# FFN gate and up projections with the weights stationary and the operand's two parts streamed side by side

## The chip, the cores and the metric

The kernel runs on one core of a Trainium2 chip. The metric is the device time of one execution, in microseconds (us). Three executions of the kernel before took 1697.11 to 1703.02 us, median 1700.94 us. The profiled execution, from which all rows below come, took 1709.87 us, with a span of 1708.0 us from the first to the last instruction.

## The reference, cut to what matters

256 tokens of 1024 channels go through two stacks of two layers each. The first stack's layer is an FFN, a mixer and a second FFN; the second stack's layer is a mixer and an FFN. So there are six FFNs. All of them compute, with `D = 1024` and `D_FF = 2816`:

```
def rms_norm(x, g):
    y = x * lax.rsqrt(jnp.mean(x * x, axis=-1, keepdims=True) + 1e-6)
    return y * g
def swiglu(x, w_in, w_out):
    gu = x @ w_in                      # 1024 x 5632
    g, u = jnp.split(gu, 2, axis=-1)
    return (jax.nn.silu(g) * u) @ w_out  # 2816 x 1024
x = x + 0.5 * swiglu(rms_norm(x, norm), w_in, w_out)   # factor 1 in the second stack
```

## The kernel before, in words

**Precision.** Every large product is made of three matmuls of the type fp32r. An operand a is split into a high part (a rounded copy) and a low part (what the copy lacks). The product of a and w is then a_hi w_hi + a_hi w_lo + a_lo w_hi (`product`, L1417; its three matmuls are L1420, L1421 and L1422).

**Weights.** They come as units of 128 x 2048 elements (1 MB) into three slots of `raw`, by SyncE's queue (`load`, L446, two DMAs to a unit). ScalarE makes the high part of a unit (`refill`, L688, one ACTIVATE, L693) and VectorE the low part (`refill`, L997, one TENSOR_TENSOR, L1000). TensorE then uses the unit and counts it in `unit_done`; a refill waits for that count and for the landing. A load into `raw` waits for the low part of the unit before (`w_lo_ready`).

**An FFN.** It has eleven steps, each for 256 of the 2816 hidden channels. A step uses three units: two hold the 256 gate and the 256 up columns for 512 input channels each (slots 2 and 0), the third 256 rows of the down weights (slot 1). In the kernel before the tokens are stationary: for each of two tiles of 128 tokens, each of eight chunks of 128 input channels is loaded as `xTh` or `xTl`, and 512 columns of weights (256 gate, 256 up) are streamed past. That is 48 matmuls of 512 columns to a step (`full_block`, L1453). The result lies in one PSUM bank per token tile, tokens on the partitions, so that the norm's factor `rstd` is one scalar per partition. ScalarE forms silu of the gate half (`silu`, L730, L731), VectorE multiplies it by the up half (`product`, L1040, L1042). The result must then be transposed for the down product: four transposes on TensorE (`turn`, L1486, L1491), into the first bank of the pair. ScalarE makes the high part of that (`product_hi`, L739, L741) and VectorE the low part (`product_lo`, L1049, L1052). The down product is 24 matmuls of 512 columns into the four banks `acc` (`down`, L1498; for the last step `last_down`, L1510).

**Order.** It is written out by hand on each engine. TensorE runs: the first gate and up block, then for j = 0 to 9 the block of step j+1 and the down product of step j, then the last down product. The turn of step j+1 is issued half way through the down product of step j. The banks `pg` form two pairs, which the steps use in turn. ScalarE and VectorE go through the same steps with their refills in between. At the start of an FFN ScalarE and VectorE also finish the operand `xT`, and ScalarE waits for `rstd` from GpSimd. SyncE issues the loads in the order of use, with some other loads at fixed steps of the first stack's first FFNs: before step 6 it loads the attention bias (`attention_bias`), to which GpSimd then adds a mask in sixteen instructions (L631).

Of the kernel before, what the change touches and what calls it, by code (L numbers as in the profile page):

```python
# [20 lines left out]
F32 = mybir.dt.float32  # L21
# [113 lines left out]
class Signals:  # L135


    def __init__(self, sem):
# [37 lines left out]
        self.ffn_sum_done = sem("ffn_sum_done")  # L176
        self.silu_ready = sem("silu_ready")
        self.act_ready = sem("act_ready")
        self.actT_tr = sem("actT_tr")
        self.actT_hi = sem("actT_hi")  # L180
        self.actT_lo = sem("actT_lo")
# [103 lines left out]
def build(nc, a, out):  # L285

    with ExitStack() as ctx:
        def sb(name, shape, dt=F32):
            return ctx.enter_context(nc.sbuf_tensor(name, shape, dt))

        def psum(name):
            return ctx.enter_context(nc.psum_tensor(name, [P, BANK], F32))
# [28 lines left out]
        rstd = sb("rstd", [P, TT])  # L321
        rfin = sb("rfin", [P, TT])
        rnext = sb("rnext", [P, TT])
        consts_a = sb("consts_a", [P, CA_COLS])

        shared = sb("shared", [P, TT * NA_H * T])
# [13 lines left out]


        sg, act = area(12288, TT, FB), area(12800, TT, FB)
        squared = area(12288, D)


# [46 lines left out]
        spread = nc.dram_tensor("rpb_spread", (GRID_W, DEPTH * NA_H, NA_DR * GRID_W), F32, kind="Internal").ap()  # L392

        causal = consts_b[:, CB_CAUSAL:CB_CAUSAL + T]

# [4 lines left out]
        def f32(ap):  # L400
            return ap.bitcast(F32)
# [32 lines left out]
        def unit(slot, rnd):  # L434

            return SLOTS * rnd + slot
# [246 lines left out]
        def _(act_e):  # L683
# [43 lines left out]
            def ffn(rnd, f, n, o):  # L727
                begin(rnd, n, o)

                def silu(t, par):  # L730
                    act_e.activation(sg[:, t, :], pg[par][t][:, 0:FB], ACT.Silu, scale=rstd[:, t:t + 1]).then_inc(s.silu_ready, 1)  # L731

                refill(0, rnd + 1)
                act_e.wait_ge(s.ffn_t0_done, STEPS * f + 1)
                silu(0, 0)
                act_e.wait_ge(s.unit_done, unit(1, rnd) + 4)
                silu(1, 0)

                def product_hi(j, par):  # L739
                    act_e.wait_ge(s.actT_tr, STEPS * f + j + 1)  # L740
                    act_e.activation(bTh[:, 2 * par:2 * par + 2, :], pg[par][0][:, :].rearrange("p (c n) -> p c n", c=2),  # L741
                                     ACT.Copy).then_inc(s.actT_hi, 1)

                with act_e.Fori(0, (STEPS - 1) // 2) as jj:
                    for par in range(2):
                        j = 2 * jj + par
                        product_hi(j, par)
                        refill(1, rnd + j + 1)
                        act_e.wait_ge(s.ffn_t0_done, STEPS * f + j + 2)
                        silu(0, 1 - par)  # L750
                        refill(2, rnd + j + 1)
                        act_e.wait_ge(s.unit_done, unit(0, rnd + j + 1) + 4)
                        silu(1, 1 - par)
                        refill(0, rnd + j + 2)
                product_hi(STEPS - 1, 0)
# [240 lines left out]
        def _(v):  # L996
# [40 lines left out]
            def ffn(rnd, f, n, o, factor, gain=None, next_gain=None):  # L1037
                begin(rnd, n, o, gain)

                def product(t, par, j):  # L1040
                    v.wait_ge(s.silu_ready, 2 * STEPS * f + 2 * j + t + 1)
                    v.scalar_tensor_tensor(act[:, t, :], pg[par][t][:, FB:2 * FB], rstd[:, t:t + 1], sg[:, t, :],  # L1042
                                           ALU.mult, ALU.mult).then_inc(s.act_ready, 1)

                refill(0, rnd + 1)
                product(0, 0, 0)
                product(1, 0, 0)

                def product_lo(j, par):  # L1049
                    v.wait_ge(s.actT_hi, STEPS * f + j + 1)  # L1050
                    part = slice(2 * par, 2 * par + 2)
                    v.tensor_tensor(bTl[:, part, :], pg[par][0][:, :].rearrange("p (c n) -> p c n", c=2),  # L1052
                                    f32(bTh[:, part, :]), ALU.subtract).then_inc(s.actT_lo, 1)

                with v.Fori(0, (STEPS - 1) // 2) as jj:
                    for par in range(2):
                        j = 2 * jj + par
                        product_lo(j, par)
                        refill(1, rnd + j + 1)
                        product(0, 1 - par, j + 1)  # L1060
                        refill(2, rnd + j + 1)
                        product(1, 1 - par, j + 1)
                        refill(0, rnd + j + 2)
                product_lo(STEPS - 1, 0)

                def add(t, n2):
                    if t == 1 and n2 == 1:
                        v.wait_ge(s.unit_done, unit(2, rnd + STEPS - 1) + 4)
                    else:
                        v.wait_ge(s.ffn_sum_done, 3 * f + 2 * t + n2 + 1)  # L1070
                    residual(t, n2, acc[2 * t + n2], factor)

                if not next_gain:
                    for t in range(TT):
# [341 lines left out]
        def _(pe):  # L1416
# [63 lines left out]
            def ffn(rnd, f, n, o, alone):  # L1480
# [5 lines left out]
                def turn(j, par):  # L1486

                    pe.wait_ge(s.act_ready, 2 * STEPS * f + 2 * j + 2)
                    for t in range(TT):
                        for c in range(2):  # L1490
                            tr = pe.transpose(pg[par][0][:, c * T + t * P:c * T + (t + 1) * P], act[:, t, c * P:(c + 1) * P], ident[:, :])  # L1491
# [6 lines left out]
                def down(j, par, slot, r, first):  # L1498

                    pe.wait_ge(s.actT_lo, STEPS * f + j + 1)  # L1500
                    split_ready(slot, r)
                    for t in range(TT):
                        for k in range(2):
                            for n2 in range(2):
                                mm = added(t, par, slot, n2, k, first and k == 0, False)
                        if t == 0:
                            turn(j + 1, 1 - par)
                    mm.then_inc(s.unit_done, 1)

                def last_down(slot, r):  # L1510
# [15 lines left out]
                def step(j, par, amid=None, first=False):  # L1526
                    full_block((2, 0), (rnd + j, rnd + j + 1), BANK, pg[1 - par], s.ffn_t0_done, amid=amid)
                    down(j, par, 1, rnd + j + 1, first)

                step(0, 0, {(0, 1): lambda: turn(0, 0)}, first=True)  # L1530
                with pe.Fori(0, (STEPS - 3) // 2) as jj:
                    step(2 * jj + 1, 1)
                    step(2 * jj + 2, 0)
                step(STEPS - 2, 1)
                last_down(2, rnd + STEPS - 1)

            def mixer_a(l):
# [396 lines left out]
```

## Time and profile before

| | before |
|---|---|
| median of 3 executions | 1700.94 us |
| profiled execution, its span | 1709.87 us, 1708.0 us |
| VectorE, ScalarE, GpSimd busy | 55%, 47%, 6% of the span |
| transposes of the FFN (L1491) | 264, 40.5 us busy |
| splits of weight units (L693, L1000) | 277 on each engine |
| DMA engines, mean rate | 54.9% of 16 engines' span, 181 GB/s |

A busy time is the union of the instructions' records. Matmul records are longer than the distance from one matmul to the next (a matmul of 512 columns has a record of 0.39 us, and the next starts 0.227 us after it), since they are pipelined: what a matmul costs is read from the starts in the timeline, not from its record. Instructions of SyncE and the issue of DMAs are not counted as busy.

### The profile page before, as it was taken

Reading aid. Unit: us, or ns where it says so; the run is one execution under the profiler, and the core shown is the slowest. Engines: PE = TensorE matmul, PEld = TensorE weight load, DVE = VectorE, ACT = ScalarE, POOL = GpSimd, SP = SyncE. Lnnn points to the kernel's source line nnn. Section 1 sums busy time; section 2 is a strip of 40 time slices with the busy share of each in tenths; the row PEclk is TensorE's granted clock in tenths of the full one; section 3 lists DMA queues with packets and bytes.
Section 4 is the critical chain, followed back from the end, with each engine's and each line's share of the span. In section 5 each row is a group of like instructions: output and inputs, shape, how many; then the busy total and the mean of one; then the engine's idle time right before and its main releaser. Section 6 shows DMA issues by size and latency. Waiting matters only on the chain.

```text
span 1708.0 us, 20654 instructions
## 1 busy us (share of the span) xinstructions
PE 1665.7 (98%) x7760; PEld 1374.9 (80%) x7760; DVE 946.6 (55%) x843; ACT 800.4 (47%) x896; POOL 108.2 (6%) x138
## 2 busy tenths in 40 slices
PE   6998999999999998999999999989999999999998
PEld 5887887888888887888888888878888888888886
DVE  4545555575454645464556554566655556665454
ACT  4443454545444543345454444466444446554443
POOL 2010000000000002000001000031100002110000
PEclk9999999999999999999999999999999999999999
DMA  8884553356565677545345675642566564356562
GB/s 257 297 227 151 193 182 125 124 175 198 194 196 173 200 256 212 188 165 183 137 139 157 216 251 172 217 129 99 161 197 198 178 210 129 105 166 209 184 195 88
DMA packets 209179, 308.87 MB, mean 181 GB/s; under 512 B 10400, under 2 KB 153504, under 8 KB 208480
## 3 DMA queue, kind: packets, MB, share of 16 engines
q1 hardware_dynamic: 208272, 305.18, 54.9%
q0 software_dynamic: 560, 1.84, 0.4%
q8 instruction: 40, 0.66, 0.2%
q10 hardware_dynamic: 288, 1.05, 0.2%
q14 instruction: 19, 0.16, 0.0%
HBM read 306.97 MB, written 2.88 MB: 181 GB/s over the span
## 4 chain that ended last, share of the span: by engine, by line
PE 92%; DVE 3%; ACT 1%; DMA 1%; issue 1%; POOL 1%; SPq 0%; DVEq 0%; POOLq 0%; ACTq 0%
PE pg L1420 19%; PE pg L1422 19%; PE pg L1421 19%; PE acc L1420 8%; PE acc L1422 8%; PE acc L1421 8%; PE pg L1491 2%; DVE wlo L1000 2%; DMA raw<-in_ffn_w_in 1%; PE acc L1570 1%; PE pg L1433 1%; ACT whi L693 1%; PE acc L1590 1%; PE acc L1578 0%; PE acc L1610 0%
## 5 line engine op out<-in xcount | busy, mean ns | idle before, releaser
L1000 DVE TENSOR_TENSOR wlo<-raw,whi 128x2048 fp32r<-128x2048 f32 x277 | 646.3, 2334 | 522.0 <-ACT whi L693 522.0
L693 ACT ACTIVATE whi<-raw 128x2048 fp32r<-128x2048 f32 x277 | 529.5, 1914 | 355.5 <-PE acc L1422 165.7
L1420 PE MATMUL pg<-whi,xTh 128*128 128x512 f32 (+1 forms) x1456 | 578.2, 397 | 12.8 <-DVE wlo L1000 8.4
L1422 PE MATMUL pg<-whi,xTl 128*128 128x512 f32 (+1 forms) x1456 | 568.5, 390 | 0.0
L1421 PE MATMUL pg<-wlo,xTh 128*128 128x512 f32 (+1 forms) x1456 | 568.4, 390 | 0.0
L1420 PEld LDWEIGHTS pg<-whi,xTh 128*128 128x128 f32 x1456 | 274.9, 189 | 74.2 <-DVE wlo L1000 11.4
L1422 PEld LDWEIGHTS pg<-whi,xTl 128*128 128x128 f32 x1456 | 274.8, 189 | 57.2
L1421 PEld LDWEIGHTS pg<-wlo,xTh 128*128 128x128 f32 x1456 | 275.1, 189 | 54.1
L1420 PE MATMUL acc<-whi,bTh 128*128 128x512 f32 (+1 forms) x572 | 230.5, 403 | 0.0
L1422 PE MATMUL acc<-whi,bTl 128*128 128x512 f32 (+1 forms) x572 | 224.5, 392 | 0.0
L1421 PE MATMUL acc<-wlo,bTh 128*128 128x512 f32 (+1 forms) x572 | 224.0, 392 | 0.0
L731 ACT ACTIVATE work<-pg,rstd 128x256 f32<-128x256 f32 x132 | 62.1, 474 | 237.0 <-PE pg L1422 236.9
L1422 PEld LDWEIGHTS acc<-whi,bTl 128*128 128x128 f32 x572 | 108.2, 189 | 23.4
L1420 PEld LDWEIGHTS acc<-whi,bTh 128*128 128x128 f32 x572 | 108.6, 190 | 20.7 <-DVE bTl L1182 0.5
L1421 PEld LDWEIGHTS acc<-wlo,bTh 128*128 128x128 f32 x572 | 108.5, 190 | 20.5
L1042 DVE SCALAR_TENSOR_TENSOR work<-pg,rstd,work 128x256 f32<-128x256 f32 x132 | 62.9, 481 | 90.3 <-ACT work L731 90.3
L603 POOL TENSOR_TENSOR ms<-ss,eps 128x1 f32<-128x1 f32 x24 | 25.3, 1053 | 1140.9 <-ACT work L700 1140.9
L741 ACT ACTIVATE bTh<-pg 128x512 fp32r<-128x512 f32 x66 | 39.6, 601 | 81.0 <-PE pg L1491 81.0
L706 ACT ACTIVATE xTh<-pg 128x512 fp32r<-128x512 f32 x48 | 28.3, 597 | 58.8 <-PE pg L1433 58.7
L758 ACT ACTIVATE work<-acc 128x512 f32<-128x512 f32 (+2 forms) x44 | 25.2, 578 | 65.4 <-PE acc L1578 55.4
L1052 DVE TENSOR_TENSOR bTl<-pg,bTh 128x512 fp32r<-128x512 f32 x66 | 45.2, 684 | 15.3 <-ACT bTh L741 15.3
L1491 PE MATMUL pg<-ident,work 128*128 128x128 f32 x264 | 40.5, 276 | 8.6 <-DVE work L1042 8.6
(162 smaller groups left out, 1045.8 us busy)
## 6 DMA issues: line engine op xcount, KB each, us to landing
raw<-in_ffn_w_in SPq DMA_DIRECT2D x176, 512.0 KB, 4.9
raw<-in_ffn_w_out SPq DMA_DIRECT2D x88, 512.0 KB, 4.3
raw<-in_w_gate_up SPq DMA_DIRECT2D x88, 512.0 KB, 4.8
raw<-in_mix_w_in SPq DMA_DIRECT2D x64, 512.0 KB, 4.5
raw<-in_w_down SPq DMA_DIRECT2D x44, 512.0 KB, 4.2
raw<-in_w_in SPq DMA_DIRECT2D x24, 512.0 KB, 4.6
raw<-in_mix_w_o SPq DMA_DIRECT2D x16, 512.0 KB, 4.6
raw<-in_w_o SPq DMA_DIRECT2D x16, 512.0 KB, 4.2
```

The costliest lines, as they stand in the source:

```text
L603: pool.tensor_tensor(sums, mean, eps[:, 0:n], ALU.add).then_inc(ms_sem, 1)
L693: act_e.activation(whi[:, slot, :], raw[:, slot, :], ACT.Copy).then_inc(s.w_hi_ready, 1)
L706: act_e.activation(xTh[:, 4 * b:4 * b + 4, tok(t)], pg[b][t][:, :].rearrange("p (c n) -> p c n", c=4), ACT.Copy).then_inc(s.xT_hi_ready, 1)
L731: act_e.activation(sg[:, t, :], pg[par][t][:, 0:FB], ACT.Silu, scale=rstd[:, t:t + 1]).then_inc(s.silu_ready, 1)
L741: act_e.activation(bTh[:, 2 * par:2 * par + 2, :], pg[par][0][:, :].rearrange("p (c n) -> p c n", c=2), ACT.Copy).then_inc(s.actT_hi, 1)
L1000: v.tensor_tensor(wlo[:, slot, :], raw[:, slot, :], f32(whi[:, slot, :]), ALU.subtract).then_inc(s.w_lo_ready, 1)
L1042: v.scalar_tensor_tensor(act[:, t, :], pg[par][t][:, FB:2 * FB], rstd[:, t:t + 1], sg[:, t, :], ALU.mult, ALU.mult).then_inc(s.act_ready, 1)
L1052: v.tensor_tensor(bTl[:, part, :], pg[par][0][:, :].rearrange("p (c n) -> p c n", c=2), f32(bTh[:, part, :]), ALU.subtract).then_inc(s.act ...
L1420: pe.matmul(dst, xh, wh, start=first and i == 0, stop=False)
L1421: pe.matmul(dst, xh, wl, start=False, stop=False)
L1422: mm = pe.matmul(dst, xl, wh, start=False, stop=last and i == len(pairs) - 1)
L1491: tr = pe.transpose(pg[par][0][:, c * T + t * P:c * T + (t + 1) * P], act[:, t, c * P:(c + 1) * P], ident[:, :])
```

## The change

In steps 1 to 10 of each FFN the weights are stationary: 128 columns of a weight unit are loaded, and the tokens are streamed. `xTh` and `xTl` now lie side by side in one tile, so the high part of the weights meets both in one matmul of 512 columns (256 tokens high, 256 tokens low), and the low part of the weights meets `xTh` alone in one of 256 columns. A step's block is 32 matmuls of 512 columns and 32 of 256. The products come out transposed, hidden channels on the partitions, and in two partial sums (high and low tokens) that VectorE adds with a TENSOR_REDUCE. The gate's bank pair is `pg[1]` in every step and the up bank pair `pg[0]`. The norm's factor is now a row over the tokens: `rstd` goes to DRAM and comes back broadcast to all partitions; it multiplies the gate before silu, and for the up half it is applied at the residual (`rhalf` or `rstd`). Step 0 is made as before, and is the only one that is turned, into `acc[3]`. The lines below leave out the declarations of seven semaphores and unchanged code.

```
-        xTh = sb("xTh", [P, KC, T], F32R)
-        xTl = sb("xTl", [P, KC, T], F32R)
+        xT = sb("xT", [P, KC, 2 * T], F32R)
+        xTh, xTl = xT[:, :, 0:T], xT[:, :, T:2 * T]
...
-        pg = [[psum(f"pg{i}{t}") for t in range(TT)] for i in range(2)]
+        pg_all = ctx.enter_context(nc.psum_tensor("pg", [P, 4, BANK], F32))
+        pg = [[pg_all[:, 2 * i + t, :] for t in range(TT)] for i in range(2)]
... ScalarE, ffn
+                    act_e.dma_start(rows_dram[f, :].rearrange("(t p) -> p t", t=TT), rstd[:, :]).then_inc(s.row_stored, LOADED)
                 refill(0, rnd + 1)
... silu of step 0, both tiles, as before
+                refill(1, rnd + 1)
+                act_e.wait_ge(s.row_stored, LOADED * (f + 1))
+                act_e.dma_start(row, bass.AP(tensor=rows_dram.tensor, offset=f * T, ap=[[0, P], [1, T]])).then_inc(s.row_landed, LOADED)
+                act_e.wait_ge(s.actT_tr, f + 1)
+                act_e.activation(bTh[:, 0:2, :], acc[3][:, :]..., ACT.Copy).then_inc(s.actT_hi, 1)
+                def step(j, par, last=False):
+                    refill(2, rnd + j)
+                    act_e.wait_ge(s.gate_scaled, (STEPS - 1) * f + j)
+                    act_e.activation(gateT, gateT, ACT.Silu).then_inc(s.silu_ready, 1)
+                    refill(0, rnd + j + 1)
+                    act_e.wait_ge(s.act_ready, (STEPS + 1) * f + 2 + j)
+                    act_e.activation(bTh[:, 2 * par:2 * par + 2, :], actT, ACT.Copy).then_inc(s.actT_hi, 1)
+                    if not last:
                         refill(1, rnd + j + 1)
... VectorE, ffn
+                def both(bank):
+                    return pg_all[:, bank:bank + 2, :].rearrange("p c (parts n) -> p c n parts", parts=2)
+                def step(j, par, last=False):
+                    refill(2, rnd + j)
+                    v.wait_ge(s.gate_done, (STEPS - 1) * f + j)
+                    v.tensor_reduce(gateT, both(2), AX.X, ALU.add).then_inc(s.gate_summed, 1)
+                    v.wait_ge(s.gate_summed, (STEPS - 1) * f + j)
+                    v.tensor_tensor(gateT, gateT, row.unsqueeze(1).to_broadcast([P, 2, T]), ALU.mult).then_inc(s.gate_scaled, 1)
+                    v.wait_ge(s.unit_done, unit(0, rnd + j) + 4)
+                    v.tensor_reduce(actT, both(0), AX.X, ALU.add).then_inc(s.up_summed, 1)
+                    v.wait_ge(s.up_summed, (STEPS - 1) * f + j)
+                    v.wait_ge(s.silu_ready, (STEPS + 1) * f + 2 + j)
+                    v.tensor_tensor(actT, actT, gateT, ALU.mult).then_inc(s.act_ready, 1)
+                    refill(0, rnd + j + 1)
                     v.wait_ge(s.actT_hi, STEPS * f + j + 1)
+                    v.tensor_tensor(bTl[:, part, :], actT, f32(bTh[:, part, :]), ALU.subtract).then_inc(s.actT_lo, 1)
+                    if not last:
                         refill(1, rnd + j + 1)
... TensorE, ffn
+                def gate_up(j, begins=False):
+                    banks = (pg[1][0], pg[1][1], pg[0][0], pg[0][1])
+                    for half, slot, r in ((0, 2, rnd + j - 1), (1, 0, rnd + j)):
+                        split_ready(slot, r)
+                        for c in range(4):
+                            if half == 0 and begins and c == 2:
+                                turn()
+                            if half == 0 and not begins and c == 0:
+                                pe.wait_ge(s.gate_summed, (STEPS - 1) * f + j - 1)
+                            if half == 0 and not begins and c == 2:
+                                pe.wait_ge(s.up_summed, (STEPS - 1) * f + j - 1)
+                            for i in range(4):
+                                wh, wl = weights(slot, i * BANK + c * P, P)
+                                pe.matmul(banks[c], wh, xT[:, 4 * half + i, :], start=half == 0 and i == 0, stop=False)
+                                mm = pe.matmul(banks[c][:, 0:T], wl, xTh[:, 4 * half + i, :], start=False, stop=half == 1 and i == 3)
+                            if half == 1 and c == 1:
+                                mm.then_inc(s.gate_done, 1)
+                        mm.then_inc(s.unit_done, 1)
+                gate_up(1, begins=True)
+                down(0, 0, 1, rnd + 1, True)
+                ... for j = 1 to 9: gate_up(j + 1), down(j, ...)
                 last_down(2, rnd + STEPS - 1)
```

## Rows read from the trace of the kernel before

**Rows 1.** The page: busy time of TensorE, and its shares of the chain of waits.
```profile
PE 1665.7 (98%) x7760; PEld 1374.9 (80%) x7760; DVE 946.6 (55%) x843; ACT 800.4 (47%) x896; POOL 108.2 (6%) x138
...
PE 92%; DVE 3%; ACT 1%; DMA 1%; issue 1%; POOL 1%; SPq 0%; DVEq 0%; POOLq 0%; ACTq 0%
```

**Rows 2.** The waits of TensorE: who waited for whom, total us, times, longest.
```profile
PE pg L1491 <- DVE work L1042: 8.6, 2, 4.3
PE pg L1420 <- DVE wlo L1000: 8.4, 7, 2.7
```

**Rows 3.** Timeline of ScalarE, first FFN: start, duration, instruction, idle before it.
```profile
45.93 0.60 ACT L741 ACTIVATE bTh<-pg 128x512 fp32r<-128x512 f32 x1 [0.88 <-PE pg L1491]
...
113.14 0.60 ACT L741 ACTIVATE bTh<-pg 128x512 fp32r<-128x512 f32 x1 [0.87 <-PE pg L1491]
```

**Rows 4.** Timeline of TensorE around one turn.
```profile
45.06 0.39 PE L1422 MATMUL acc<-whi,bTl 128*128 128x512 f32 x1
45.29 0.60 PE L1491 MATMUL pg<-ident,work 128*128 128x128 f32 x4
45.65 0.48 PE L1420 MATMUL acc<-whi,bTh 128*128 128x512 f32 x1
45.96 0.40 PE L1421 MATMUL acc<-wlo,bTh 128*128 128x512 f32 x1
```

**Rows 5.** Timeline of TensorE: fp32r streams of 512 and of 384 columns.
```profile
39.17 0.39 PE L1420 MATMUL pg<-whi,xTh 128*128 128x512 f32 x1
...
42.34 0.39 PE L1422 MATMUL pg<-whi,xTl 128*128 128x512 f32 x1
...
1139.77 0.33 PE L1420 MATMUL acc<-whi,bTh 128*128 128x384 f32 x1
...
1140.81 0.39 PE L1420 MATMUL acc<-whi,bTh 128*128 128x512 f32 x1
```

**Rows 6.** Timeline of TensorE: fp32r of 64 columns, then f32 of 256.
```profile
1177.52 0.27 PE L1420 MATMUL pg<-whi,bTh 64*128 64x64 f32 x1
...
1179.20 0.27 PE L1420 MATMUL pg<-whi,bTh 64*128 64x64 f32 x1
...
1195.80 3.67 PE L1803 MATMUL pg<-work,shared 128*128 128x256 f32 x16
```

**Rows 7.** Timelines around GpSimd's mask, and the window with the clock (PEclk).
```profile
101.13 2.29 DVE L1000 TENSOR_TENSOR wlo<-raw,whi 128x2048 fp32r<-128x2048 f32 x1 [2.73 <-ACT whi L693]
...
120.00 11.17 POOL L631 TENSOR_TENSOR shared<-shared,consts_a 128x256 f32<-128x256 f32 x16 [95.30 <-DMA shared<-rpb_spread]
...
126.02 7.30 DVE L1000 TENSOR_TENSOR wlo<-raw,whi 128x2048 fp32r<-128x2048 f32 x1 [3.68 <-ACT whi L693]
...
133.77 1.11 PE L1491 MATMUL pg<-ident,work 128*128 128x128 f32 x4 [4.30 <-DVE work L1042]
...
131.60:138.50 6.90, 4.73 (x14) 3.91 (x15) 4.92 (x4) 0.60 (x1) 0.00 (x0) 0.51 0.56 177
```

**Rows 8.** VectorE's groups by form: count, busy us, mean ns, idle before.
```profile
L1000 DVE TENSOR_TENSOR wlo<-raw,whi 128x2048 fp32r<-128x2048 f32 x277 | 646.3, 2334 | 522.0 <-ACT whi L693 522.0
...
L1131 DVE TENSOR_REDUCE na_neg<-work 128x2 f32<-128x512 f32 x16 | 11.0, 686 | 0.6
```

**Rows 9.** Timelines of TensorE and ScalarE at the end of a down product.
```profile
48.50 0.39 PE L1420 MATMUL pg<-whi,xTh 128*128 128x512 f32 x1
...
48.70 1.92 ACT L693 ACTIVATE whi<-raw 128x2048 fp32r<-128x2048 f32 x1 [2.17 <-PE acc L1422]
```

**Rows 10.** Timelines at the starts of FFNs: the first turn, and an issue by ScalarE.
```profile
7.56 0.33 ACTq L979 DMA_DIRECT2D x<-in_x  x1
...
33.67 0.87 DVE L1042 SCALAR_TENSOR_TENSOR work<-pg,rstd,work 128x256 f32<-128x256 f32 x2
...
392.21 0.87 DVE L1042 SCALAR_TENSOR_TENSOR work<-pg,rstd,work 128x256 f32<-128x256 f32 x2
...
394.46 0.60 PE L1491 MATMUL pg<-ident,work 128*128 128x128 f32 x4
```

More of the change, by code:

```diff
@@ L728, in ffn @@
                 begin(rnd, n, o)
-                def silu(t, par):
-                    act_e.activation(sg[:, t, :], pg[par][t][:, 0:FB], ACT.Silu, scale=rstd[:, t:t + 1]).then_inc(s.silu_ready, 1)
+                with nc.allow_non_contiguous_dma(reason="one value of each partition"):
+                    act_e.dma_start(rows_dram[f, :].rearrange("(t p) -> p t", t=TT), rstd[:, :]).then_inc(s.row_stored, LOADED)
                 refill(0, rnd + 1)
-                act_e.wait_ge(s.ffn_t0_done, STEPS * f + 1)
@@ L735, in ffn @@
[L735 to L747, printed above, removed]
-                        refill(1, rnd + j + 1)
[L749 to L754, printed above, removed]
@@ L755, in ffn @@
-                product_hi(STEPS - 1, 0)
+                for t in range(TT):
+                    if t == 0:
+                        act_e.wait_ge(s.ffn_t0_done, f + 1)
+                    else:
+                        act_e.wait_ge(s.unit_done, unit(1, rnd) + 4)
+                    act_e.activation(sg[:, t, :], pg[0][t][:, 0:FB], ACT.Silu, scale=rstd[:, t:t + 1]).then_inc(s.silu_ready, 1)
+                refill(1, rnd + 1)
+                act_e.wait_ge(s.row_stored, LOADED * (f + 1))
+                act_e.dma_start(row, bass.AP(tensor=rows_dram.tensor, offset=f * T, ap=[[0, P], [1, T]])).then_inc(s.row_landed, LOADED)
@@ L757, in copy @@
+                with act_e.Fori(0, (STEPS - 3) // 2) as jj:
+                    step(2 * jj + 1, 1)
+                    step(2 * jj + 2, 0)
+                step(STEPS - 2, 1)
+                step(STEPS - 1, 0, last=True)
             def copy(dst, src, sem, scale=1.0):
@@ L1045, in ffn @@
                 refill(0, rnd + 1)
-                product(0, 0, 0)
-                product(1, 0, 0)
-                def product_lo(j, par):
+                for t in range(TT):
+                    v.wait_ge(s.silu_ready, (STEPS + 1) * f + t + 1)
+                    v.tensor_tensor(act[:, t, :], pg[0][t][:, FB:2 * FB], sg[:, t, :], ALU.mult).then_inc(s.act_ready, 1)
+                refill(1, rnd + 1)
+                v.wait_ge(s.actT_hi, STEPS * f + 1)
+                v.tensor_tensor(bTl[:, 0:2, :], acc[3][:, :].rearrange("p (c n) -> p c n", c=2), f32(bTh[:, 0:2, :]),
+                                ALU.subtract).then_inc(s.actT_lo, 1)
@@ L1064, in ffn @@
-                product_lo(STEPS - 1, 0)
+                    v.tensor_tensor(bTl[:, part, :], actT, f32(bTh[:, part, :]), ALU.subtract).then_inc(s.actT_lo, 1)
+                    if not last:
+                        refill(1, rnd + j + 1)
+                with v.Fori(0, (STEPS - 3) // 2) as jj:
+                    step(2 * jj + 1, 1)
+                    step(2 * jj + 2, 0)
+                step(STEPS - 2, 1)
+                step(STEPS - 1, 0, last=True)
+                scale = rstd
+                if factor != 1.0:
+                    v.wait_ge(s.rhalf_ready, f + 1)
+                    scale = rhalf
@@ L1524, in last_down @@
                                     transposes(0, n2, o + 1)
[L1526 to L1530, printed above, removed]
+                gate_up(1, begins=True)
+                down(0, 0, 1, rnd + 1, True)
                 with pe.Fori(0, (STEPS - 3) // 2) as jj:
-                    step(2 * jj + 1, 1)
-                    step(2 * jj + 2, 0)
-                step(STEPS - 2, 1)
+                    for odd in range(2):
+                        j = 2 * jj + odd + 1
+                        gate_up(j + 1)
+                        down(j, 1 - odd, 1, rnd + j + 1, False)
+                gate_up(STEPS - 1)
+                down(STEPS - 2, 1, 1, rnd + STEPS - 1, False)
                 last_down(2, rnd + STEPS - 1)
```

39 lines of the change are left out of this document (19 added, 20 removed).

## The prediction

> **What bounds the kernel now.** I read the page's busy shares first: TensorE is busy 98% of the span, and the chain that ended last runs through it for 92% [rows 1]. Then its waits, to see what the other 2% are: two long waits of a turn for VectorE, and 8.4 us for weight splits [rows 2]. VectorE and ScalarE are half idle. So this change is worth what it does to the distances between matmuls, plus the few waits that it removes or makes. Third, the timeline of one step. ScalarE's copy after a turn comes at 45.93 and, four copies later, at 113.14: a step takes 67.21 / 4 = 16.80 us [rows 3], and nothing but TensorE's own instructions fills it: 72 matmuls and one turn.
>
> **The turns.** Without a turn the matmul at 45.96 would come two distances of 0.227 us after the one at 45.06. It comes 0.90 us after: a turn costs 0.90 - 0.454 = 0.446 us, of which four transposes are 0.36 and the rest is a late second matmul behind them [rows 4]. Ten of eleven turns in each of six FFNs go: 60 x 0.446 = 26.8 us saved. A mean matmul of the step is then (16.80 - 0.446) / 72 = 0.2271 us.
>
> **The block.** Before it is 48 matmuls of 512 columns, 48 x 0.2271 = 10.90 us. After it is 32 of 512 and 32 of 256: the same 24,576 columns, but 64 instructions and 64 weight loads. What counts is what an instruction costs beside its columns. In the stream of 512 columns 14 matmuls start in the 3.17 us from 39.17 to 42.34 (fourteen distances), 0.2264 each; in that of 384, six in 1.04 us, 0.1733 each [rows 5]. The difference is 0.0531 us for 128 columns, 0.415 ns a column (2.4 GHz), and 0.2264 - 512 x 0.000415 leaves 0.014 us that does not shrink with the columns. So a matmul of 256 columns should take 0.106 + 0.014 = 0.120 us.
>
> No row shows an fp32r matmul of 256 columns. From below, its weight load bounds it: the matmuls of 64 columns, each with its own 128 columns of weights, come every 1.68 / 15 = 0.112 us [rows 6]. From above, the f32 matmuls of 256 columns come every 3.67 / 16 = 0.229 us at most [rows 6]. I take 0.120: it is the line through two fp32r rows, and it lies above the load's 0.112. The block is 32 x (0.2271 + 0.120) = 11.11 us, 0.21 more than before; 60 blocks cost 12.5 us. With 0.112 they would give back 2.9 us, with 0.229 cost 221.8 us.
>
> Of the weight load, the Trainium skill ("TensorE: Matmul & The Clock Gate", section "LDWEIGHTS (loading the stationary operand)") says that it takes the columns over 1.2 GHz, 107 ns for 128. The trace agrees (0.112). The same page ("Back-to-back issue gap") says that in a stream of loads and matmuls both count, 81 ns against 56 at 128 columns, 25 ns more than the columns explain. By it a 256 column matmul would be an estimated 134 ns, and the sum below 1712 instead of 1685; the 384 column row, with 14 ns over, speaks against it.
>
> **Is VectorE in time?** A new step is 11.11 + 24 x 0.2271 = 16.56 us. VectorE's work in it: three splits of 2.33; two reduces of 1024 elements, each 0.686 + 512 x (2.334 - 0.686) / 1536 = 1.24 [rows 8]; three operations of 512 elements at 0.69: 11.5 us. ScalarE: three splits of 1.92 and two of 0.60, 7.0 us [rows 3, 9]. Laid out from a block's start at 0: half 0 ends at 5.55, ScalarE splits slot 2 from 5.8 (it starts 0.2 after the next matmul does [rows 9]) and VectorE to 10.0; gate sum to 11.3, scaled at 11.9; up sum to 13.1, product at 13.8; slot 0 split to 16.7, low part of the product to 17.4; slot 1, free at 16.6, split to 21.0. TensorE needs the gate sum at 16.6, the up sum at 19.3, slot 0 at 22.1, slot 1 and the product at 27.7: at least 5 us of slack everywhere, though the banks are no longer used in turn. The units' loads have 12 us each. In the loop I charge nothing. The cover is that slack; if it went, each us late would cost 60.
>
> **The last step.** Here there is no next block, only one down product of 5.45 us between the up half and `last_down`. The low part, behind the split of the next stage's slot 0, is ready at 17.4 in the layout above, and the block ended at 11.1: 6.2 us later by the unrounded numbers. TensorE waits 0.75 us, six times 4.5 us. With faster operations 0; with reduces of double time 2.4 each, 14.
>
> **The stall that goes.** GpSimd's mask takes 11.17 us from 120.00, and the split on VectorE that begins at 126.02 takes 7.30 instead of 2.29: it ends 2.1 us after GpSimd does [rows 7]. Behind it stands the product, and the turn waits to 133.77, 4.46 us. After that TensorE shows a mean granted clock of 0.51 from 131.6 to 138.5 [rows 7], its lower level of 1.2 GHz; 4.6 us of work at half rate lose 2.3 more. This happens in both layers: 13.5 us. After the change the split at fault is that of slot 2. GpSimd starts 16.6 us after the split that ended at 103.42 (101.13 + 2.29), which comes 4.5 us into a block; that puts the mask at 4.5 to 15.7 us of the next one. The slot 2 split, due at 7.8, ends at 17.8, the gate sum at 19.1, and TensorE stands at 16.6: a wait of 2.5 us. I take it as too short to bring the clock down, being near the 2.7 of [rows 2] and far from 4.3 (if it does, 2.3 each on top). Twice 2.5 = 5 stays, 8.5 us are saved (0 to 13.5). The Trainium skill ("SBUF — State Buffer", section "SBUF: two separate sides") says that a VectorE operation with two SBUF inputs and a GpSimd operation exclude each other for a whole instruction. The row agrees and more: the split lost the whole rest of the mask. By it the scaling and the products, now from SBUF alone, would be held too; they stand behind the same split.
>
> **The first step.** Step 0 stays, but its turn comes after 16 matmuls of the new block (8 x 0.347 = 2.78 us) instead of 18 old ones (4.09), 1.31 earlier. The products end at 393.08, the turn comes at 394.46 [rows 10]: 1.38 of slack becomes 0.07. ScalarE's new store stands ahead of its refill; an issue takes 0.33 [rows 10]. About 0.35 us late, six times 2.1 us (0 to 6; in the first FFN the product ends at 34.54 anyway [rows 10]). The row's way through DRAM has over 6 us of cover in slot 2's refill.
>
> **Sum:** -26.8 + 12.5 + 4.5 - 8.5 + 2.1 = -16.2 us. Against the profiled execution's 1709.9 us that is 1693.7. That execution was 8.9 us over the median shown; on the median's scale it is 1700.9 - 16.2 = 1684.7 us, and this is the number that I give.
>
> **Rivals.**
> (a) Forecast: as above, 1685, its own range 1677 to 1693. 0.58.
> (b) The change of length costs: from the first transpose's start to that of the second matmul behind them are 0.67 us [rows 4], where four transposes at 0.11 (their 0.60 less one record of 0.27, over three) and one matmul of 0.227 would be 0.66 to 0.67. These rows can hide 10 ns; 10 ns on each of 1920 matmuls of 256 columns are 19 us: 1704, no change. 0.10.
> (c) The other side: the weight load is exposed. During 256 columns (0.107) a load of 0.112 must be made; if the fixed 0.014 is paid twice, 0.134 each: 1920 x 0.014 = 27 us more, 1712, slower. It decides from 0.128 on (16.2 / 1920 over 0.120). For it: the load is longer than the columns. Against: at 64 columns it costs 0.112 and no more [rows 6]. 0.10. With the f32 rate of 0.229 it would be 1894: 0.04.
> (d) The sums are slow: reading two partial sums apart takes double, 2.4 us a reduce. The loop's slack holds it, the last steps cost 9.6 more and the mask's waits 2.4: 1697. 0.08.
> (e) It gains more: 0.112 for 256 columns (-15.4) and no wait beside the mask (-5): 1664. 0.10.
>
> **Chances.** A difference of 0.3%, 5 us, is about what a measurement of this kernel tells from none. Faster by more: (a), (e) and half of (d), 0.72. Within: (b) and the rest of (d), 0.14. Slower: (c), 0.14. The range from 1665 to 1711 leaves out the f32 rate and the far ends of (c) and (e).
>
> **What would show it.** Distances of the 256 column matmuls in the timeline: 0.120 right, 0.112 (e), 0.130 (b), 0.134 (c). A distance of steps of 16.56 us. 24 transposes in the turns instead of 264. Waits of TensorE for the low part of the product six times, each under 1 us; at the mask's steps a wait of 2 to 3 us for the gate sum, and a clock that stays up. Reduces of 1.24 us. It would be wrong if TensorE waited in each step for the sums, or if the steps were longer than 16.80.

## The result: slower by 1.3%

The changed kernel takes 1725.2 us (median of 4 runs, 1716.7 to 1728.0) where the kernel before takes 1700.1 beside it (4 runs, 1697.1 to 1703.0): a ratio of 1.013 with a 95% interval of 1.010 to 1.016. The two medians lie 25.1 us apart, which would be 1.5%; by the ratio it is 22 us. The forecast was 1684.7, the range ended at 1711. The changed kernel's profiled execution, 1716.7 us with a span of 1714.9, is the fastest of the four, so what it shows is rather less than what the other runs pay.

The page of the changed kernel: busy time, the chain of waits by engine, and the groups of the new matmuls and of the sum over the two halves of a bank.

```profile
PE 1665.3 (97%) x8480; PEld 1396.5 (81%) x8480; DVE 1108.3 (65%) x967; ACT 776.2 (45%) x836; POOL 123.6 (7%) x138
...
PE 79%; DVE 7%; DMA 7%; ACT 3%; issue 2%; POOL 1%; DVEq 0%; SPq 0%; POOLq 0%; ACTq 0%
...
L1541 PE MATMUL pg<-xT,whi 128*128 128x512 f32 x1920 | 684.5, 400 | 11.5 <-DVE work L1076 11.5
...
L1542 PE MATMUL pg<-xT,wlo 128*128 128x256 f32 x1920 | 540.6, 282 | 0.0
...
L1076 DVE TENSOR_REDUCE work<-pg 128x512 f32<-128x1024 f32 x60 | 73.1, 1218 | 0.0
```

Against [rows 1], TensorE is busy as long as before, though 240 transposes are gone, and the chain left it: its share fell from 92% to 79%, and VectorE, the DMAs and ScalarE hold 17% where they held 5%. That is where to look. The waits of TensorE, in the columns of [rows 2], name the engine at the end of it:

```profile
PE pg L1541 <- DVE work L1076: 11.5, 5, 3.3
PE pg L1455 <- DVE wlo L1018: 4.8, 6, 1.6
...
PE acc L1455 <- DVE bTl L1087: 2.7, 6, 0.5
PE acc L1525 <- DVE work L1063: 2.0, 4, 1.4
```

The two turns that waited 8.6 us beside GpSimd's mask are gone. A wait for the gate sum, L1076, came instead, in five of six FFNs. VectorE itself was idle before it. Timelines of ScalarE, VectorE and TensorE at the start of the second FFN, each with its idle time in brackets, and the window with TensorE's clock behind it:

```profile
382.05 0.46 ACTq L744 DMA_DIRECT2D rstd_rows<-rstd  x1
...
393.04 0.34 ACTq L755 DMA_DIRECT2D work<-rstd_rows  x1
393.42 0.60 ACT L757 ACTIVATE bTh<-acc 128x512 fp32r<-128x512 f32 x1 [4.94 <-DMA rstd_rows<-rstd]
...
401.41 2.29 DVE L1018 TENSOR_TENSOR wlo<-raw,whi 128x2048 fp32r<-128x2048 f32 x1 [6.67 <-DMA work<-rstd_rows]
403.62 1.22 DVE L1076 TENSOR_REDUCE work<-pg 128x512 f32<-128x1024 f32 x1
...
404.89 0.50 PE L1541 MATMUL pg<-xT,whi 128*128 128x512 f32 x1 [2.73 <-DVE work L1076]
...
406.30:409.80 3.50, 3.50 (x13) 3.02 (x12) 2.82 (x3) 3.50 (x3) 0.00 (x0) 0.51 0.64 215
```

This is the row's way through DRAM. ScalarE issues the store at 382.05; it lands 11 us later, and ScalarE stood in its queue for it, 4.94 us before its copy. Only then can the load be issued, at 393.04, and it takes 8.1 us more. VectorE waits for it in front of a weight split, not in front of the operation that reads the row, so the split, 2.29 us, and the sum, 1.22 us, come behind it, and TensorE finds its bank unread. TensorE then works at full speed for 1.4 us, and after that the granted clock is 0.51 for 3.5 us, the level of 1.2 GHz. The rows of DMA issues (KB each, median us from issue to landing) and the waits for the two transfers show that it is the rule:

```profile
work<-rstd_rows ACTq DMA_DIRECT2D x6, 128.0 KB, 8.1
...
rstd_rows<-rstd ACTq DMA_DIRECT2D x6, 1.0 KB, 11.1
```

```profile
  DVE wlo L1018: 33.2, 6
```

```profile
  ACT bTh L757: 26.8, 5
...
DMA to landing us min/median/max: 9.5/11.1/13.8
```

VectorE stood 33.2 us at the load, ScalarE 26.8 us at the store, whose 1 KB is two values of each partition. In TensorE's timeline the distances at these places are 3.12, 3.69, 2.55 and 1.35 (in one FFN, the 1.35 at the low part behind ScalarE's late copy), 2.55 and 1.55 us; less a common distance of 0.227 in each they are 13.4 us. In three of the blocks behind them the clock fell to half; the blocks took 1.50, 1.23 and 1.50 us more than the others, 4.2 in all.

The second place is the loop. Timeline of ScalarE in the second FFN: its copy after each product, as in [rows 3].

```profile
437.57 0.61 ACT L765 ACTIVATE bTh<-work 128x512 fp32r<-128x512 f32 x1
...
555.05 0.61 ACT L765 ACTIVATE bTh<-work 128x512 fp32r<-128x512 f32 x1
```

Seven steps in 117.48 us: 16.78 each, where the forecast had 16.56 and the kernel before 16.80. From start to start of TensorE's blocks or turns it is 16.793 against 16.803. TensorE waits for no sum there, and the turn is gone; what it cost was eaten inside the block and behind it. Timeline of TensorE in it:

```profile
633.13 0.40 PE L1541 MATMUL pg<-xT,whi 128*128 128x512 f32 x1
633.36 0.28 PE L1542 MATMUL pg<-xT,wlo 128*128 128x256 f32 x1
633.48 0.40 PE L1541 MATMUL pg<-xT,whi 128*128 128x512 f32 x1
633.72 0.28 PE L1542 MATMUL pg<-xT,wlo 128*128 128x256 f32 x1
633.84 0.40 PE L1541 MATMUL pg<-xT,whi 128*128 128x512 f32 x1
634.08 0.28 PE L1542 MATMUL pg<-xT,wlo 128*128 128x256 f32 x1
634.19 0.40 PE L1541 MATMUL pg<-xT,whi 128*128 128x512 f32 x1
```

Three pairs take 1.06 us, 0.353 each. Read from the starts of 54 blocks, a matmul of 512 columns holds the next one back by 0.236 us (0.227 before, throughout the block), one of 256 columns by 0.117. The sum, 0.353, was forecast as 0.347. A block is 11.29 us against 10.88. The 24 matmuls of the down product behind it take 5.503 us, where 24 distances of 0.2267 would be 5.441.

### The profile page after: what moved, and what is told of

It is laid out like the page before. It is cut to its first block, busy times and chain, and to the rows that moved or that the text cites. A ratio compares the mean times of both kernels' runs of the same rounds, so it can differ in the third digit from the quotient of the medians.

```text
span 1714.9 us, 22033 instructions
## 1 busy us (share of the span) xinstructions
PE 1665.3 (97%) x8480; PEld 1396.5 (81%) x8480; DVE 1108.3 (65%) x967; ACT 776.2 (45%) x836; POOL 123.6 (7%) x138
## 4 chain that ended last, share of the span: by engine, by line
PE 79%; DVE 7%; DMA 7%; ACT 3%; issue 2%; POOL 1%; DVEq 0%; SPq 0%; POOLq 0%; ACTq 0%
PE pg L1541 23%; PE pg L1542 12%; PE acc L1455 7%; PE acc L1457 7%; PE acc L1456 7%; PE pg L1455 6%; PE pg L1457 5%; PE pg L1456 5%; DVE wlo L1018 3%; DMA rstd_rows<-rstd 3%; DMA work<-rstd_rows 2%; ACT whi L706 2%; DMA raw<-in_ffn_w_in 1%; PE acc L1621 1%; PE acc L1641 1%
## 5 line engine op out<-in xcount | busy, mean ns | idle before, releaser
L1541 PE MATMUL pg<-xT,whi 128*128 128x512 f32 x1920 | 684.5, 400 | 11.5 <-DVE work L1076 11.5
L1542 PE MATMUL pg<-xT,wlo 128*128 128x256 f32 x1920 | 540.6, 282 | 0.0
L1541 PEld LDWEIGHTS pg<-xT,whi 128*128 128x128 f32 x1920 | 362.8, 189 | 102.2 <-DVE work L1076 13.6
L1542 PEld LDWEIGHTS pg<-xT,wlo 128*128 128x128 f32 x1920 | 364.7, 190 | 2.1
L1455 PE MATMUL pg<-whi,xT 128*128 128x512 f32 (+1 forms) x496 | 203.5, 410 | 10.0 <-DVE wlo L1018 4.8
L1457 PE MATMUL pg<-whi,xT 128*128 128x512 f32 (+1 forms) x496 | 194.7, 393 | 0.0
L1456 PE MATMUL pg<-wlo,xT 128*128 128x512 f32 (+1 forms) x496 | 194.4, 392 | 0.0
L762 ACT ACTIVATE work<-work 128x512 f32<-128x512 f32 x60 | 38.0, 633 | 281.9 <-DVE work L1078 281.9
L1455 PEld LDWEIGHTS pg<-whi,xT 128*128 128x128 f32 x496 | 94.5, 191 | 33.4 <-DVE wlo L1018 7.3
L1457 PEld LDWEIGHTS pg<-whi,xT 128*128 128x128 f32 x496 | 94.5, 191 | 19.4
L1456 PEld LDWEIGHTS pg<-wlo,xT 128*128 128x128 f32 x496 | 94.7, 191 | 16.7
L1076 DVE TENSOR_REDUCE work<-pg 128x512 f32<-128x1024 f32 x60 | 73.1, 1218 | 0.0
L1080 DVE TENSOR_REDUCE work<-pg 128x512 f32<-128x1024 f32 x60 | 73.0, 1217 | 0.0
```

Of the source, the lines that this page charges most:

```text
L762: act_e.activation(gateT, gateT, ACT.Silu).then_inc(s.silu_ready, 1)
L1076: v.tensor_reduce(gateT, both(2), AX.X, ALU.add).then_inc(s.gate_summed, 1)
L1080: v.tensor_reduce(actT, both(0), AX.X, ALU.add).then_inc(s.up_summed, 1)
L1455: pe.matmul(dst, xh, wh, start=first and i == 0, stop=False)
L1456: pe.matmul(dst, xh, wl, start=False, stop=False)
L1457: mm = pe.matmul(dst, xl, wh, start=False, stop=last and i == len(pairs) - 1)
```

## The experiments

Times are medians in us; each ratio is to the kernel before, run on the same chip. Edits are against the changed kernel unless said.

**e1: no way through DRAM.** Both transfers and the waits for them are gone; the row is a tile of ones.

```diff
-                act_e.dma_start(rows_dram[f, :]..., rstd[:, :]).then_inc(s.row_stored, LOADED)
-                act_e.wait_ge(s.row_stored, LOADED * (f + 1))
-                act_e.dma_start(row, bass.AP(...)).then_inc(s.row_landed, LOADED)
-                v.wait_ge(s.row_landed, LOADED * (f + 1))
+            v.memset(row[:, :], 1.0)
```

> The changed kernel without the way of the norm's factor through DRAM: both DMAs and the wait for them are left out, and the gate is multiplied by a row of ones (so the norm's factor is left out of the gate). Theory R (the row arrives late in the first step of an FFN, and TensorE then waits for the gate sum and falls to its lower clock): five of six waits for the gate sum and three of the falls go, 13 + 5 = 18 us of the profiled execution of the changed kernel and somewhat more of its slower ones: 1697 to 1705 us, no wait of TensorE over 1 us in the FFNs. Rival S (the distances of the matmuls in the new block are all of it): within 4 us of the changed kernel's 1725.

Measured: 1698.6, before 1698.5, ratio 1.0008 (0.9994 to 1.0022). The loss of 1.3% is gone. The window in which the changed kernel had waited, in the changed kernel and in e1 (its length, the engines' busy times PE, PEld, DVE, ACT and POOL, then clock, DMA share and GB/s):

```profile
390.00:410.00 20.00, 17.27 (x82) 14.38 (x82) 9.38 (x8) 6.81 (x6) 0.00 (x0) 0.91 0.52 161
...
390.00:410.00 20.00, 20.00 (x108) 17.09 (x107) 12.52 (x11) 8.71 (x6) 0.00 (x0) 1.00 0.69 219
```

In e1 TensorE is busy for all 20 us at the full clock. What e1 leaves out is more than the wait, so e3 makes the row in another way.

**e3: the row made on the chip.** VectorE writes the diagonal of each token tile (the identity times the factor of each partition), TensorE multiplies it by a tile of ones, which adds up each column and gives every partition the whole row; VectorE copies it out.

```diff
+                for t in range(TT):
+                    last = v.tensor_scalar(row[:, tok(t)], ident[:, :], rstd[:, t:t + 1], None, ALU.mult)
+                last.then_inc(s.row_stored, 1)
...
+                v.tensor_copy(row, acc[2][:, 0:T]).then_inc(s.row_stored, 1)
...
+                    pe.matmul(acc[2][:, 0:T], ones[:, :], row, start=True, stop=True).then_inc(s.row_landed, 1)
```

> The changed kernel with the row made on the chip: VectorE scales the unit matrix by the factor (two operations of 128 columns), TensorE multiplies it by a matrix of ones behind the turn (256 columns of f32), VectorE copies it from PSUM; the whole reference is computed. Theory R: as with the row of ones, plus about 0.5 us of TensorE in each FFN: 1700 to 1708. Rival S: 1725 to 1729.

Measured: 1700.5, before 1698.5, ratio 1.0017 (1.0004 to 1.0030). The wait for L1076 has no row left. Its timeline of VectorE, at the place shown above:

```profile
387.61 0.47 DVE L1062 TENSOR_SCALAR work<-ident,rstd 128x128 f32<-128x128 f32 x2
...
390.90 0.42 DVE L1066 COPY work<-acc 128x256 f32<-128x256 f32 x1
```

The row is there 3.7 us after the first of these begins, not 19 us after a store is issued. Against the kernel before, the changed kernel lost 25.1 us by the medians and e3 loses 2.0: the way through DRAM costs 23 us of the timed runs, or 19 by the two ratios (1.0130 less 1.0017). Their intervals, 0.67% to 1.59% apart at their extremes, allow 11 to 27.

**e2 and e4: groups of four.** Each bank gets its four matmuls of 512 columns, then its four of 256, so a block changes length 16 times instead of 64. e2 is that alone. e4 has it with e3's row, and in the last step both engines do the product's parts before they split the next stage's slot.

```diff
                             for i in range(4):
-                                wh, wl = weights(slot, i * BANK + c * P, P)
+                                wh, _ = weights(slot, i * BANK + c * P, P)
                                 pe.matmul(banks[c], wh, xT[:, 4 * half + i, :], start=half == 0 and i == 0, stop=False)
+                            for i in range(4):
+                                _, wl = weights(slot, i * BANK + c * P, P)
                                 mm = pe.matmul(banks[c][:, 0:T], wl, xTh[:, 4 * half + i, :], start=False, stop=half == 1 and i == 3)
```

> The changed kernel with the four 512 column matmuls of a bank first and the four 256 column matmuls behind them, instead of in turn. Theory A (a change of length costs: 0.236 + 0.117 for a pair instead of 0.227 + 0.120): inside a group 0.227 and 0.120, a block is 11.1 instead of 11.3 us and the kernel 10 to 12 us faster, 1713 to 1715. Rival F (each matmul costs its columns plus a fixed 0.016 us in this form, in any order): the pair stays at 0.353 and the time within 3 us of 1725. Rival L (a row of 256 column matmuls is bound by the weight load): 256 columns at 0.112, a block at 10.9 us, 1704 to 1708.

> The row on the chip, the grouped order, and in the last step of each FFN the product's two parts ahead of the next stage's split. By theories R and A: 1725 less 20 (row), less 11 (order), less 6 x 0.6 (the wait ahead of the last down product) = 1690, faster than the kernel before's 1700. By R and F: 1701. By S alone: 1721.

Measured: e2 1715.2, ratio 1.0094 (1.0074 to 1.0113); e4 1690.4, ratio 0.9955 (0.9942 to 0.9967), faster than both kernels. In e4's timeline, behind four of 256 columns the four of 512 hold the next one back by 234, 235, 229 and 232 ns; the first four of a block, behind a down product of 512 columns, by 227 each. A block is 11.20 us and a step 16.687 instead of 16.793, 6.4 us over 60 steps; by the ratios e2 gained 6.1. e2 and e4 ran on one chip: the row and the last step together are 24.8 us there.

**e5: the low part as long as the high one.** The second matmul of each pair also streams 512 columns, which adds the product of the two low parts; then no length changes at all, with the same 64 instructions and loads.

```diff
-                                mm = pe.matmul(banks[c][:, 0:T], wl, xTh[:, 4 * half + i, :], ...)
+                                mm = pe.matmul(banks[c], wl, xT[:, 4 * half + i, :], ...)
```

> The changed kernel with 512 columns in both matmuls of a pair: the low part of the weights meets the tokens' low part too, so the result holds one more small product. It asks where the 6 to 9 ns come from that a 512 column matmul of the new block takes beyond 0.227 us. Theory P (256 column matmuls leave the 512 column ones behind them late): with no 256s left all distances in the block are 0.227, a block 64 x 0.227 = 14.5 us, the kernel 1725 + 60 x 3.2 = 1917 us. Rival W (weights stationary and tokens streamed is itself slower): 0.233 to 0.236, a block 15.0 us, the kernel 1947.

Measured, one run: 1882.9, before 1696.6. Timeline of TensorE:

```profile
60.17 0.39 PE L1541 MATMUL pg<-xT,whi 128*128 128x512 f32 x1
60.39 0.39 PE L1542 MATMUL pg<-xT,wlo 128*128 128x512 f32 x1
...
61.53 0.39 PE L1541 MATMUL pg<-xT,whi 128*128 128x512 f32 x1
```

Six distances in 1.36 us: 0.227 again. So neither the number of instructions and loads nor the order of the operands makes 0.236; the presence of 256 columns between does. The time was expected at 1917 and came out 34 us lower, and that tells of the row: the two transfers are as slow as before, and VectorE stands at the load for 33.1 us, but TensorE waits for no gate sum at all, nor ahead of the last down product. A block of 14.5 us covers what one of 11.3 left open. Steps of 19.946 us instead of 16.803 bring the 1696.6 of the kernel before to 1885 with nothing charged for the row, and 1882.9 were measured. VectorE's timeline and the waits for the two transfers in e5:

```profile
430.88 2.29 DVE L1018 TENSOR_TENSOR wlo<-raw,whi 128x2048 fp32r<-128x2048 f32 x1 [7.14 <-DMA work<-rstd_rows]
...
  DVE wlo L1018: 33.1, 6
  ACT bTh L757: 23.6, 5
```

**e6: the kernel before without GpSimd's mask**, against [rows 7]: its 16 additions in each layer are left out.

```diff
-            (the loop of GpSimd's mask additions)
+            pool.sem_inc(s.bias_masked, TT * NA_H)
```

> The kernel before with GpSimd's sixteen mask additions left out (so the attention of the first stack is unmasked). The forecast priced the stall beside them at 13.5 us of the profiled execution of before: without it 1685 to 1688 if every execution has it, and 1698 less 3 to 9 if only some have. If the stall costs nothing in the timed runs: 1698.

Measured: 1695.6 (12 runs), before 1696.6 (29 runs, 1691.4 to 1707.9), ratio 0.9986 (0.9967 to 1.0005). The interval allows a gain of 5.6 us at most, so the 13.5 us that the mask cost in the profiled execution are not in the usual one. In the changed kernel's profile the two engines met in another way (timelines of GpSimd and VectorE):

```profile
120.32 18.71 POOL L644 TENSOR_TENSOR shared<-shared,consts_a 128x256 f32<-128x256 f32 x16 [94.75 <-DMA shared<-rpb_spread]
...
125.06 2.32 DVE L1018 TENSOR_TENSOR wlo<-raw,whi 128x2048 fp32r<-128x2048 f32 x1 [5.11 <-ACT whi L706]
...
131.75 2.79 DVE L1018 TENSOR_TENSOR wlo<-raw,whi 128x2048 fp32r<-128x2048 f32 x1
```

GpSimd's mask stretched from 11.17 to 18.71 us, and VectorE's splits took 2.3 to 2.8 us beside it. TensorE did not wait. It is the same in both layers of all nine profiled kernels of the new form. Whether the unprofiled executions of the kernel before met in this way too isn't known.

**e7, e8, e9: how long the groups, and what else they move.** All have e3's row and e4's last step. e8 keeps the pairs; e7 takes the sixteen of 512 columns of a half, then its sixteen of 256; e9 does so in the first half alone, and takes eight and eight in the second half and in the first block, so that the turn and the end of the gate come earlier. The order of e9:

```diff
+                        for pair in ((range(4),) if whole else (range(0, 2), range(2, 4))):
+                            for c in pair:
...                              (four matmuls of 512 columns each)
+                            for c in pair:
...                              (four matmuls of 256 columns each)
+                            if half == 0 and begins and pair[0] == 0:
                                 turn()
```

> Row on the chip, the last step's order, and in each half of a block all sixteen 512 column matmuls ahead of the sixteen 256 column ones (instead of four and four, 1690). Theory P with a recovery after about four matmuls: 12 of 16 at 0.227, a block 11.1 us instead of 11.2, 1684. If the 512s after a 256 stay at 0.233 as long as the block lasts: 1690.

> Row on the chip and the last step's order, with the matmuls in turn as in the changed kernel. Ahead of the last down product TensorE waited 0.61 us in each FFN; if that is the order's whole price, 1700.5 - 3.7 = 1697, and what is left to the 1690 of all three, 6 us, is the grouping's. If instead the split moved behind is late for the next stage, 1700.

> Row on the chip, the last step's order, and groups as long as the other engines allow: sixteen and sixteen matmuls in half 0, eight and eight for the gate and then for the up banks in half 1 (so that the gate is done as early as in the changed kernel), the turn of step 0 behind the first eight and eight. With sixteen everywhere a block took 11.11 us against 11.20 with fours, but the kernel was 4.5 us slower, which theory G puts on the gate that was done 1.8 us later in the last block and on the turn that came 1 us too early. By G a block takes 11.13 us and the waits are those of the groups of four: 1690.4 - 60 x 0.07 = 1686. If long groups cost in another place: 1690 to 1695.

Measured: e8 1697.2, ratio 1.0004 (0.9987 to 1.0020), under e3 by 3.2 us in the medians and by 2.2 in the ratios, whose intervals overlap; e7 1694.9, ratio 0.9986 (0.9970 to 1.0002); e9 1686.5, ratio 0.9955 (0.9940 to 0.9969). The timeline of TensorE in e7, equal instructions in a row merged:

```profile
133.37 3.79 PE L1551 MATMUL pg<-xT,whi 128*128 128x512 f32 x16
137.00 2.08 PE L1555 MATMUL pg<-xT,wlo 128*128 128x256 f32 x16
138.91 3.82 PE L1551 MATMUL pg<-xT,whi 128*128 128x512 f32 x16
```

Sixteen behind a stream of 512 columns take 3.63 us, 0.227 each; those of 256 columns take 1.91, 0.1195 each. The starts show that inside this stream every one from the third on is at 120 ns, and that behind it the next ones of 512 columns come at 233, 236, 228, 233 and 231 ns, and then at 227. A block is 11.106 us, the forecast's 11.11, and a step 16.573, 0.114 less than e4's. But e7 gained less than e4. Its waits of TensorE, and its timeline of TensorE where the next stage begins, show why:

```profile
PE acc L1533 <- DVE work L1063: 5.3, 6, 2.2
...
205.58 0.60 PE L1476 MATMUL pg<-ident,xn 128*128 128x128 f32 x4
207.08 0.50 PE L1463 MATMUL pg<-whi,xT 128*128 128x512 f32 x1 [0.90 <-DVE xT L1032]
```

With sixteen first, the turn of step 0 stands behind eight matmuls of 512 columns, 1.82 us, and comes before its product is ready, in all six FFNs (e4: once, 0.5 us); and the gate's half of the last block ends later, so VectorE finishes the next stage's operand later, and the matmul that reads it starts 1.17 us after the last transpose instead of 0.65, in five stages. That is 4.8 and 2.6 us, against 6.8 gained in the steps. In this execution TensorE also ran at half the clock from 33.1 to 36.5 us, right behind the first turn's wait of 2.2 us. e9 took most of this away: its later turns come without a wait and the 1.17 is 0.69. One wait is left in its profile, in the first FFN:

```profile
PE acc L1533 <- DVE work L1063: 4.1, 1, 4.1
```

That execution took 1691.0 us, 4.5 over e9's median and the slowest of its six, so the wait may not stand in the others. e9 came in at 1686.5, the time expected, but the kernel before took 1693.5 on that chip, where it had taken 1698.5 beside e4; by the ratio e9 is as fast as e4, not faster. That the longer groups are worth more than four is not shown.

## Why the prediction was wrong, step by step

**The row's way through DRAM is the step that failed.** "The row's way through DRAM has over 6 us of cover in slot 2's refill" priced it at nothing. It costs 19 to 23 us (e3 against the changed kernel), nearly all of the loss. The prediction treated as one thing what is a chain: store, landing, ScalarE's wait, issue, load, VectorE's wait, then a split and a sum. The two transfers alone are 19 us at the medians. It also named nothing queued behind the two waits: a copy behind ScalarE's, a split of 2.29 us and the sum behind VectorE's, 3.5 us more in front of TensorE. It counted 12 us for each of the units' loads and none for either of these. The prediction also held a wait of 2.5 us to be too short to bring the clock down; here a wait of 2.3 us (2.55 between two starts) was once followed by half the clock (at 1255 us) and once not (at 956). The changed kernel's own profile explains 17.6 us of it, 13.4 of waiting and 4.2 of clock; the rest is in runs that were not profiled and stays inferred. The Trainium skill ("DMA: Bandwidth & Descriptors", section "Rules for kernel authors") says that a last dimension that isn't contiguous becomes one descriptor for each element. The trace agrees: the changed kernel moved 1728 more packets under 512 B than e9, 288 for each of six rows, and 272 of these, of 4 bytes each, belong to the store. The Trainium skill, on the same page ("Anatomy of one DMA — SWDGE (gpsimd) path"), has a fixed cost of about 2.0 us for a transfer that GpSimd issues; these two were issued by ScalarE, and if it held for them it would make an estimated 4 us. The runs show 19, beside weight loads that keep the DMA engines 56% busy. The 4-byte packets themselves are the smaller part of the store: in the second FFN the first begins 3.0 us after the issue and the last 4.3 us after it, and the landing comes at 11.0. In all six FFNs 2.7 to 8.1 us pass between the last packet and the landing. What fills them was not tried.

**The block was right in kind, half in size.** "The line through two fp32r rows" gave 0.120 for 256 columns, and inside a run of them it is 0.120 (e7). The term lacked what the mixture does: 0.236 and 0.117 instead of 0.227 and 0.120. 60 blocks cost 60 x 0.41 = 24.6 us where 12.5 were forecast, and the matmuls of the down product behind each block are late too, 0.062 us in all, 3.7 us over 60 steps. This is rival (b)'s mechanism with 6 ns a pair where it had put 10. It isn't a fixed fee for each change: the matmuls of 256 columns in it are even 3 ns early, and about five later ones of 512 are late, some 20 ns in all for each change behind a run of sixteen (e7). With pairs, no more than one of 512 columns stands between two changes, and the price stays at 6. Rival (c), the exposed load, falls: 0.120 in a run is no 0.134. Rival (d) falls with reduces of 1.218 us against 1.24.

**The turns were right in kind, a little small.** [rows 4] show only two matmuls behind a turn, and the ones after them are late too. In the median of all 66 turns of the kernel before, with the nine matmuls behind a turn counted in, it costs 0.483 us, not 0.446: 29.0 us instead of 26.8. With +24.6 and +3.7 the loop gives 0.7 us back, which is the 16.803 against 16.793. So the trace of the kernel before already held matmuls of 512 columns that come late behind shorter ones.

**The last step was right in kind**, forecast as 0.75 us in each FFN. Timeline of TensorE in the changed kernel:

```profile
199.24 0.39 PE L1457 MATMUL acc<-whi,bTl 128*128 128x512 f32 x1
200.09 0.50 PE L1455 MATMUL acc<-whi,bTh 128*128 128x512 f32 x1 [0.45 <-DVE bTl L1087]
```

The mean distance here is 0.84 instead of 0.227: six times 0.61 is 3.7 us, forecast 4.5. In e8 this distance is gone in all six FFNs; its gain in time, 2.2 to 3.2 us, is not clear of the noise.

**The mask was sized from one execution.** "8.5 us are saved" was read from the profiled execution and subtracted from the median too. In the profiled executions the whole 13.5 is gone, since the wait of 2.5 us that was to stay beside the mask in each layer didn't come (no such row in TensorE's waits). e6 puts the whole mask at some 1 us of 1697, at most 5.6. That the profiled run was 8.9 us over the median was in the working and should have been read as the sign of it.

**VectorE in time, and the first step.** In the loop no wait of TensorE for a sum shows. In five FFNs the first turn came 0.30 to 0.39 us late, as forecast (0.35); in e1 and e3, without ScalarE's store ahead of the refill, these five are gone. In the first FFN, where nothing was forecast, it came 1.5 us late, but a wait of 2.3 us for a weight split that the kernel before had there in its profile is gone.

**The sum again, from what was measured:** the loop -0.7 (turns -29.0, blocks +24.6, down products behind them +3.7), the last step +3.7, the first turns +1.7 and the first FFN -0.8, the mask 0: that makes +3.9 without the row. e3, which has neither the row nor the late turns but has two more matmul instructions in each FFN, shows +2.0 (0.7 to 5.1 by its interval). With the row's 19 to 23 it is 23 to 27; 22 (ratio) to 25.1 (medians) were measured. The row's price is itself taken from the changed kernel's time, so this closing tests the other terms alone. Two sizes of the row don't lean on that time: the 17.6 us of the profile, and the 24.8 between e2 and e4 less 3.7 for the last step, 21. Groups of four gave 8.3 us between e8 and e4 by their ratios, where steps shorter by 0.106 make 6.4; the intervals of the two ratios hold the difference.

## What to carry to other kernels

A value that goes to DRAM and back is two transfers, two waits in two engines' queues, and everything queued behind both; write that chain down with a duration for each link, and ask whether a matmul with ones can make the row instead. When a change mixes instructions of different length in TensorE's stream, the price of the mixture is its own term, and grouping equal lengths is worth trying (steps shorter by 0.106 us of 16.793 with groups of four), as long as the turn and the sums that wait on a group's end don't move back. A stall that a profiled execution shows can be counted against the median only if the profiled execution stands at it; one that stands above it has to be suspected of holding exactly that stall.

## What the runs showed of the hardware that was not expected

- Behind matmuls of 256 columns, the next ones of 512 start 233, 236, 228, 233 and 231 ns apart and only then at 227, in e7 at all 60 such places inside blocks and within 1 ns; the first two of 256 behind 512 come at 113 and 119 ns, the rest at 120. The weight load's record in a run of 256 columns is 192 ns long and begins 2 to 3 ns after the start of the matmul before. What in the engine makes the pattern is open.
- Storing 256 values of 4 bytes took 9.5 to 13.8 us, longer than reading the row back to 128 partitions, 128 KB, 5.6 to 8.5 us. Of the store, 2.7 to 8.1 us lie behind its last packet.
- GpSimd's mask and VectorE's split met in two ways: 11.17 us with a split held for 7.30 [rows 7], and 18.71 us with splits of 2.3 to 2.8. The Trainium skill ("SBUF — State Buffer", section "SBUF: two separate sides") has the one that starts first hold the other for a whole instruction; the second way agrees with it: an addition of 0.73 us takes 2.8 beside a split. The first, where one split lost the whole rest of a mask of 16 additions, does not.
